# First block's slots from 34 one-column products, and the first expert's up weights split in the attention's end

## What is computed

```python
def hierarchical_moe(h, w_rg, w_re, w_g, w_u, w_d):
    ...
    order = jnp.argsort(flat_e)
    counts = jnp.bincount(flat_e, length=N_EXPERTS)
    padded = (counts + ROW_BLOCK - 1) // ROW_BLOCK * ROW_BLOCK
    padded_start = jnp.cumsum(padded) - padded
    dest = padded_start[sorted_e] + jnp.arange(A) - start[sorted_e]
    row_tok = jnp.full((P,), T, jnp.int32).at[dest].set(flat_tok[order])
    row_w = jnp.zeros((P,), jnp.float32).at[dest].set(flat_w[order])
    ...
    def expert_block(args):
        xe, e = args
        return (jax.nn.silu(xe @ w_g[e]) * (xe @ w_u[e])) @ w_d[e]
    yb = lax.map(expert_block, (xb, block_e))
    out = zeros.at[row_tok].add(yb * row_w[:, None])
```

## Times and the profile before

| | us |
|---|---|
| median of 3 runs | 2157.6 (2156.3 to 2159.7) |
| the profiled execution, own time | 2158.2 |
| its span | 2156.5 |
| PE busy | 2078.7 (96%) |
| DVE busy | 1602.6 (74%) |
| ACT busy | 1258.3 (58%) |
| the expert stage begins | 1293.52 after the span's start |

### The profile page before, as it was taken

The page is one execution under the profiler, slowest core; times in us unless marked ns, Lnnn a source line. Parts: engine busy times, 40 slices in busy tenths (PEclk is TensorE's granted clock), DMA queues, the critical chain, the costliest instruction groups (busy, mean ns, idle before and its releaser), DMA issues. The chain is left out here.

```text
span 2156.5 us, 40174 instructions
## 1 busy us (share of the span) xinstructions
PE 2078.7 (96%) x13523; PEld 1754.6 (81%) x13524; DVE 1602.6 (74%) x2056; ACT 1258.3 (58%) x2199; POOL 768.8 (36%) x697
## 2 busy tenths in 40 slices
PE   8999999998899999899999979999999999999998
PEld 6888888886787887688888767888888888888887
DVE  3799999997676667867878868698698466466644
ACT  5322433337677777867767646687687465456643
POOL 1111445564566555645545453122122111111211
PEclk9999999998999999999999999999999999999999
DMA  7564334336433242423232119999899878677851
GB/s 227 179 206 157 119 125 151 118 117 180 121 101 111 84 135 84 119 77 113 72 116 84 55 72 333 357 328 366 299 373 372 268 233 278 198 223 262 285 161 34
DMA packets 211949, 393.18 MB, mean 182 GB/s; under 512 B 54925, under 2 KB 81933, under 8 KB 211821
## 3 DMA queue, kind: packets, MB, share of 16 engines
q1 hardware_dynamic: 198285, 357.42, 48.0%
q0 software_dynamic: 13536, 34.12, 6.8%
HBM read 315.42 MB, written 91.23 MB: 189 GB/s over the span
## 5 line engine op out<-in xcount | busy, mean ns | idle before, releaser
L2663 DVE TENSOR_TENSOR p_w_lo<-p_raw,p_w_hi 128x1024 fp32r<-128x1024 f32 (+1 forms) x196 | 330.5, 1721 | 134.3 <-ACT p_w_hi L2455 134.2
L2253 POOL TENSOR_TENSOR late<-late,p_past 128x1024 f32<-128x1024 f32 (+4 forms) x166 | 308.6, 1860 | 321.5 <-DVE p_past L2097 321.2
L819 DVE SCALAR_TENSOR_TENSOR p_ut<-p_ut,p_cw 128x512 f32<-128x512 f32 (+1 forms) x480 | 329.3, 764 | 0.0
L2455 ACT ACTIVATE p_w_hi<-p_raw 128x2048 fp32r<-128x2048 f32 (+1 forms) x150 | 271.6, 1842 | 62.1 <-PE p_up L2547 53.3
L2097 DVE TENSOR_TENSOR_SCAN p_past<-p_keep,p_past,p_one 128x513 f32<-128x513 f32 (+1 forms) x196 | 225.9, 1193 | 77.4 <-ACT p_keep L1897 76.0
L1897 ACT ACTIVATE p_keep<-p_zp 128x512 f32<-128x512 f32 (+3 forms) x326 | 158.6, 546 | 105.3 <-PE p_zp L1764 94.2
L2547 PE MATMUL p_gp<-p_w_hi,p_xt_hi 128*128 128x256 f32 x736 | 214.3, 291 | 0.0
L490 PE MATMUL p_pj<-p_w_hi,p_xt_hi 128*128 128x512 f32 x512 | 205.7, 402 | 4.2 <-DVE p_xt_lo L795 2.4
L2547 PE MATMUL p_gp<-p_w_lo,p_xt_hi 128*128 128x256 f32 x736 | 206.4, 280 | 0.0
L2547 PE MATMUL p_gp<-p_w_hi,p_xt_lo 128*128 128x256 f32 x736 | 206.4, 280 | 0.0
L490 PE MATMUL p_pj<-p_w_hi,p_xt_lo 128*128 128x512 f32 x512 | 201.0, 393 | 0.0
(11 more groups left out here) (318 smaller groups left out, 4973.9 us busy)
## 6 DMA issues: line engine op xcount, KB each, us to landing
p_raw<-in_w_up SPq DMA_DIRECT2D x96, 512.0 KB
p_raw<-in_w_gate SPq DMA_DIRECT2D x96, 512.0 KB
p_raw<-in_w_down SPq DMA_DIRECT2D x96, 512.0 KB
late<-in_w_up SPq DMA_DIRECT2D x32, 512.0 KB
late<-in_w_gate SPq DMA_DIRECT2D x32, 512.0 KB
late<-in_w_down SPq DMA_DIRECT2D x32, 512.0 KB
wide_raw<-in_w_in SPq DMA_DIRECT2D x56, 256.0 KB, 3.9
wide_raw<-in_x SPq DMA_DIRECT2D x17, 512.0 KB, 5.0
```

The costliest lines, as they stand in the source:

```text
L819: dve.scalar_tensor_tensor(dst, src, cw[:, a, j:j + 1], dst, ALU.mult, ALU.add).then_inc(tap_done, 1)
L2253: pool.tensor_tensor(mine, mine, past_rows[:, u % NP, 0:n, 2:2 + w], ALU.mult).then_inc(a_done, 1)
L2455: act.activation(part(w_hi, p, wide), ring(n, wide), ACT.Copy).then_inc(whi_done, wide)
L2663: dve.tensor_tensor(part(w_lo, p, wide), ring(n, wide), part(w_hi, p, wide).bitcast(F32), ALU.subtract).then_inc(wlo_done, wide)
```

## The change

The change has these parts.

- SBUF: a tensor `keys` is kept through all three phases. The projection holds `w_hi` and `xt_lo` in it, the attention its keys (`kt`), the experts group 0 of the split weights (`first_up.hi`, `first_up.lo`) and `xt_hi`, `xt_lo`. Other tensors of the attention move in memory, and the first query loads of the attention (`load_q`) are issued later. Some semaphores are merged.
- In the attention's end, SP loads the first expert's four up pieces into the end of `v_sb` once all weighted values are done, ACT copies the high parts and DVE subtracts the low parts. The expert stage no longer loads or splits these four.
- `in_one`: one column for each of the 34 pairs, the token number where the choice is the first expert's first block (`same` is 0), else 0. 34 products with it give the first block's token numbers (`one_i`), and gather 1 uses them. The columns of the table are built afterwards.
- Four of the ten late homes are made by DVE; all ten have memory of their own (`rest_home`).
- TensorE's order: the one-column products, 24 table products, turning of the first rows, 8 products of `keep_warm`, the last ten table products. The 3 products at the start and 22 of `keep_warm` go.
- DVE makes the first `xt_lo` before the last ten columns. POOL clears `yo` after gather 1, and gather 2 waits for the slot list. The 13th weight piece waits for the last table product too.

```diff
@@ phase_attend, first_loads and first_gain
-            for n in range(2):
+            for n in range(3):
                 load_k(sp, 0, n)
-                load_q(sp, n)
-            load_k(sp, 0, 2)
 
         def first_gain(sp):
+            load_q(sp, 0)
             sp.dma_start(gq[:, :], io["q_norm_g"]).then_inc(gq_in, 16)
             for done in ended.conv:
                 sp.wait_ge(done, 16)
+            load_q(sp, 1)
             load_mix(sp, 0)
@@ phase_attend, sync, scalar, vector
+        lead_hi_step, lead_lo_step = {5: (0, 2), 6: (2, 4)}, {5: (0, 1), 7: (1, 4)}
...
             for s in range(-AHEAD, steps + 6):
+                if s == end + 4:
+                    sp.wait_ge(av_done, end)
+                    for n in range(LEAD):
+                        sp.dma_start(lead_raw(n).rearrange("p (k f) -> p k f", k=2),
+                                     io["w_up"][n * 2 * P:(n + 1) * 2 * P, :].rearrange("(k p) f -> p k f", p=P)
+                                     ).then_inc(lead_in, 16)
...
+                for n in range(*lead_hi_step.get(s - end, (0, 0))):
+                    act.wait_ge(lead_in, 16 * LEAD)
+                    act.wait_ge(z_done, base[end])
+                    act.activation(lead.hi[:, n, :], lead_raw(n), ACT.Copy).then_inc(lead_hi, 1)
...
+            def lead_rest(lo, hi):
+
+                for n in range(lo, hi):
+                    dve.wait_ge(lead_hi, n + 1)
+                    dve.tensor_tensor(lead.lo[:, n, :], lead_raw(n), lead.hi[:, n, :].bitcast(F32),
+                                      ALU.subtract)
...
+                lead_rest(*lead_lo_step.get(s - end, (0, 0)))
@@ phase_moe, SP
+                    if isinstance(i, int) and n < LEAD:
+                        sp.sem_inc(raw_in[n], 16)
+                        continue
...
                     elif n == PIECES:
                         sp.wait_ge(gathered, 16)
+                        sp.wait_ge(spread, NC)
@@ phase_moe, PE
-            for _ in range(3):
-                pe.matmul(dp[:, 0, :], late.all[:, 0:P], late.all[:, 0:4 * P], start=True, stop=True)
+            pe.wait_ge(in_one_done, 1)
             for n, (k, r) in enumerate(choices):
...
+                m = at_home(n)
+                last = pe.matmul(gp[:, 1, 0:1], homes[n][0:m, :], in_one[0:m, k, r:r + 1], start=(n == 0),
+                                 stop=(n == NC - 1))
+            last.then_inc(one_ps, 1)
+            table_of(0, 2 * EARLY)
...
-            pe.wait_ge(whi_done, 1)
-            keep_warm(22)
             pe.wait_ge(ident_done, 2)
             first_x(1)
             second_x(1)
             keep_warm(8)
+            table_of(2 * EARLY, NC)
             pe.wait_ge(table_done, 1)
@@ phase_moe, DVE
+            tt(same[:, :, :], picks.expert, late.hi, ALU.add)
...
+            dve.wait_ge(consts, 8)
+            dve.scalar_tensor_tensor(in_one[:, :, :], same[:, :, :], 0.0, vw[:, :, :, 0], ALU.is_equal,
+                                     ALU.mult).then_inc(in_one_done, 1)
+            for n in range(2 * LAST - DH, 2 * LAST):
+                k, r = rest_of[n]
+                dve.tensor_scalar(rest_homes[n], late.iota, late.row[:, k, r:r + 1], None,
+                                  ALU.is_equal).then_inc(row_two, 1)
             starts(late.hot, 0, EARLY)
...
-            dve.wait_ge(consts, 8)
+            dve.wait_ge(one_ps, 1)
+            link(dve.tensor_scalar(one_f[:, :], gp[:, 1, 0:1], pad[:, 0:1], None, ALU.add))
+            link(dve.tensor_copy(one_i[:, :], one_f[:, :]))
+            dve.sem_inc(one_done, 1)
             columns(0, 2 * EARLY)
...
+            x_rest(1)
             columns(2 * EARLY, NC)
@@ phase_moe, POOL
-            pool.wait_ge(slots_done, 1)
+            pool.wait_ge(one_done, 1)
...
-                at = slots[:, 1, 0:1]
+                at = one_i[:, 0:1]
...
             gather(1)
+            pool.memset(yo[:, :], 0.0).then_inc(zero_yo, 1)
             pool.wait_ge(table_done, 1)
             end = pool.value_load(table[0:1, 1, NE - 1:NE], min_val=NE, max_val=NBL - 2)
+            pool.wait_ge(slots_done, 1)
             gather(2)
```

More of the change, by code:

```diff
@@ L77, in home, with __init__ @@
         return self.all[:, n * P:(n + 1) * P]
+class Lead:
+    def __init__(self, keys):
+        wide = KT * C
+        self.hi = keys[:, 0:wide].rearrange("p (k f) -> p k f", k=LEAD)
+        self.lo = keys[:, wide:2 * wide].rearrange("p (k f) -> p k f", k=LEAD)
+        self.xt_hi, self.xt_lo = (keys[:, 2 * wide + n * D:2 * wide + (n + 1) * D].rearrange("p (k f) -> p k f", k=KT)
+                                  for n in range(2))
 class Programs:
@@ L1255, in attention_jobs, with phase_attend @@
     return placed, where, first, last, user
-def phase_attend(nc, io, scr, picks, shared, late, ended):
+def phase_attend(nc, io, scr, picks, shared, late, ended, wide_keys, lead):
     with ExitStack() as ctx:
@@ L2329, in phase_moe @@
         GP = PIECES // 3
[L2330 to L2333 removed]
+        w_hi, w_lo = [first_up.hi], [first_up.lo]
+        for group in range(1, 3):
+            sb(f"gap{group}", [P, (0, 48, 80)[group]])
             w_hi.append(sb(f"w_hi{group}", [P, GP, 2 * FF], F32R))
             w_lo.append(sb(f"w_lo{group}", [P, GP, 2 * FF], F32R))
[L2336 removed]
+        xt_hi, xt_lo = first_up.xt_hi, first_up.xt_lo
         ht_hi, ht_lo = sb("ht_hi", [P, FT, P], F32R), sb("ht_lo", [P, FT, P], F32R)
@@ L2358, in phase_moe @@
         first = sb("first", [P, 1])
+        same, in_one = sb("same", [P, 2, NT]), sb("in_one", [P, 2, NT])
+        one_f, one_i = sb("one_f", [P, 1]), sb("one_i", [P, 1], I32)
+        DH = 4
+        rest_home = sb("rest_home", [P, 2 * LAST, P])
         xtp = ps("xtp", [P, KT, P])
@@ L2384, in phase_moe @@
         choices = early + rest_of
-        rest_homes = [home[:, n * P:(n + 1) * P] for home, m in ((xg, 8), (sg, 2)) for n in range(m)]
+        rest_homes = [rest_home[:, n, :] for n in range(2 * LAST)]
         homes = [late.home(k, r) for k, r in early] + rest_homes
@@ L2641, in _ @@
             starts(hot[:, :, :, :], EARLY, NT)
+            for done in (xl_done, *h_done, *hl_done):
+                dve.sem_inc(done, 1)
+            x_rest(1)
             columns(2 * EARLY, NC)
@@ L2693, in block_of @@
                 rest(at, 4, PIECES, 2)
-            for done in (xl_done, *h_done, *hl_done):
-                dve.sem_inc(done, 1)
-            rest((0, 0), 0, 5, 1)
-            x_rest(1)
-            rest((0, 0), 5, PIECES, 1)
+            dve.sem_inc(wlo_done, LEAD)
+            rest((0, 0), LEAD, PIECES, 1)
             experts(dve, block_of)
@@ L2782, in build @@
                                                       ("wide_raw", [RAW, C], F32))))
-            project, ended = phase_project(nc, io, scr, shared, late.all)
-            attend, begin = phase_attend(nc, io, scr, picks, shared, late, ended)
+            project, ended = phase_project(nc, io, scr, shared, late.all, wide_keys[:, :])
+            attend, begin = phase_attend(nc, io, scr, picks, shared, late, ended, wide_keys[:, :], lead)
             with nc.Block() as block:
```

100 lines of the change are left out of this document (55 added, 45 removed).

## The result

The changed kernel takes 2176.7 us (median of 4 runs, 2174.2 to 2177.6), the kernel before 2157.0 beside it: a ratio of 1.0085, 95% interval 1.0069 to 1.0101. That is 19.7 us slower, where 3.2 were forecast, and outside the forecast range. The profiled execution took 2177.5 us, and its page begins with

The account below looks back on a forecast made before the run. TensorE's gapless expert products were taken as the bound, so a shifted handover moves the end equally. Adding +0.6 (attention's end) and +2.6 (stage's start to handover) to 2157.6 gave 2160.8 us, range 2156.5 to 2167.0.

Parts of the forecast that it names:

- From X to the handover: Expert stage's start: gather 1 hidden under VectorE's columns, gather 2 behind the slot list, its rows landed at X+24.0.
- X: Moment when the one-column products end in the expert stage; forecast S+12.6, break-even S+10.0.
- the handover: Where TensorE turns gather 2's rows, early in the expert stage; S+33.96 before the change, forecast X+24.0.
- The new products: One-column products at the expert stage's start: 68 passes, 27 at 0.205 and 41 at 0.116 us, 10.4 us together.
- rival 2: 25%: single columns at the expert stage's start don't raise the clock; 68 passes at 0.205 us, +7.2 us, 2164.8 us.
- S: Moment when the expert stage begins; 1293.52 in the profile before the change.
- The price at half clock: Expert stage's start: a one-column pass at 1.2 GHz takes 0.205 us, as earlier loads for 128 columns did.
- The rule that was weighed: One-column products: the skill's 107 ns load at both clock levels gives 7.3 us, whole change +0.1; sum didn't use it.
- The attention's end: Four transfers, copies and subtractions there make the last rows' scaling late: +0.6 us, between 0.2 and 3.5.
- Rival 5: 7%: in the attention's end the four pieces land late, holding ScalarE's copies and eviction; three late us give 2163.8.
- The first query loads: Attention's start: these loads move later, within 6.6 us of cover; costed at nothing, about 2 us if uncovered.
- The four pieces loaded early: Expert stage's start: removed transfers (2 MB) and fewer splits were beside TensorE's wait and give nothing.

Follow-up runs that it names:

- inc_early: Changed kernel with TensorE's first increments moved from behind 24 table products to ahead of the one-column products; ratio 1.0067 to the kernel before.
- warm_first: Changed kernel with three products of 512 columns put ahead of the one-column products; ratio 1.0096 to the kernel before.
- wide_columns: Changed kernel with each of the 34 one-column products moving its column 128 times; ratio 1.0071 to the kernel before.
- subs_behind: Changed kernel with the first of VectorE's four early subtractions moved from ahead of an eviction to the other three; ratio 1.0101 to the kernel before.
- one_bf16: Changed kernel with the 34 products reading homes as bf16 and slot values as two bf16 columns; ratio 1.0056 to the kernel before.
- mended_two: Changed kernel with early increments, bf16 products, reordered columns, only two up pieces loaded early, the other two subtracted by GpSimd; ratio 1.0018 to the kernel before.

## Why the prediction was wrong

**From X to the handover.** This is the step that failed: "Gather 1 starts 1.1 us after its slots and TensorE reads its rows 5.5 us later: X+7.2, hidden under the columns." It followed the slots and not GpSimd's other wait. The increment behind the table products was in the code, and in the kernel before it cost nothing, since gather 1 waited for later slots anyway. In the changed kernel the rows came at X+14.8, and the handover at X+33.0 and not X+24.0: 9.0 us. Of these inc_early gave back 5.6, which shows this step. It left 3.4: TensorE turned the rows at X+10.5 and not X+7.9, since it waited for VectorE's increment behind the columns (which took 7.9 us there, and 8.6 in the changed kernel, not 7.1), and gather 2 landed 0.7 us slower. That second increment is a wait that the prediction hadn't followed either.

**The new products.** 4.4 us. The sum let the clock rise 5.6 us after they began, as in the earlier trace rows; rival 2 (25%) named the case that came, and gave X = S+16.1 for 17.0. The price at half clock, 0.205 from the earlier trace rows, was 0.218. At the upper level 0.116 is 0.104 (warm_first). The rule that was weighed, one figure for both levels, did not hold: it gave X = S+9.5.

**The attention's end.** The term +0.6 was +3.2, within its own outer bound of 3.5 in the profiled run and beyond it in other kernels with the same code there (28.0 us against 23.1 in wide_columns). VectorE's three subtractions took 3.58 us where 3.5 were forecast, but they were taken as free for GpSimd: the ten homes beside them appear nowhere in the sum. The one ahead of them was to fit into VectorE's wait before the evictions; it ended behind that wait, since "four land in at most 7.7 us" was 8.9 here and 8.7 to 10.4 in the others, with a store of 0.5 MB issued before they had landed. Rival 5 (7%) foresaw the late landing, but had it hold ScalarE's eviction; what it held first was VectorE's, behind the subtraction.

**What held.** The first query loads cost nothing that shows: both kernels are at the same row at 1263.5, within 0.04 us, though executions differ there by more than that. The expert loop keeps its period. The four pieces loaded early give nothing, as forecast. And the form of the sum held: 0.6+2.6 forecast, +2.6 in the attention's end, +4.4 up to X and +9.0 behind it make 19.2, against 19.1 in the traces. Three terms erred in one direction. The text had priced rivals for two of them, one at a time, and for the largest it had none. They happened together.

**Still open.** What makes the four pieces land after 8.7 us in one execution and 10.4 in another isn't settled. Nor is the time of subs_behind beyond the sum, 3.2 us: behind the handover its profile has 827.0 us, 2.0 less than before, so a fallen clock there does not explain it. It is a difference of one profile to the medians of 4 and 15 runs. Of one_bf16's 2.0 us, 0.7 lie behind the handover and the rest is open in the same way.

## What to carry to other kernels

When a producer is moved earlier, list every wait of its consumer, not only the one that was last: a wait that was covered can stand behind much later work in another engine's program order. Price products with one moved column at the pace of their weight loads, and at the lower clock: 14.85 us of them did not raise it here. Where the values allow it, bf16 makes them small (0.041 us a product). In these traces VectorE's subtractions were not free for GpSimd, nor GpSimd's for VectorE: look at what both do in the same microseconds before either is given more.

## What the runs showed of the hardware

- A 128x128 fp32 pass with one moved column: 0.218 us at the lower clock (changed), 0.104 at the upper (warm_first); a bf16 product with two columns 0.041 at the lower clock (one_bf16).
- In warm_first the granted clock was up at 1301.2 to 1303.8 and at half again by 1305, though TensorE had no gap: only single columns were moved.
- GpSimd's ten homes of 128x128: 6.7 us alone, 10.4 beside 4.7 us of VectorE subtractions of 128x1024 fp32 (subs_behind). In the other direction one VectorE instruction whose like take 0.35 us lasted 5.64 us around two such subtractions on GpSimd of 4.66 us (mended_two).
- ScalarE took up four transfers of 0.5 MB each 8.7 (one_bf16) to 10.4 us (wide_columns) after their first issue; its first copy waits for all four.
- In the attention's end TensorE's clock stayed up where TensorE stood 1.4 us for an eviction (changed) and fell where it stood 2.85 us (wide_columns).
